# A four-layer conditioning sum in 1024-column pieces, merged weight sums, 24 more weight units by seven products, and all three short-convolution taps of two layers on ScalarE

## The reference, cut to what matters

```python
# first stack, layer i
g, u = jnp.split(h @ w_up[i], [D_FF], axis=-1)          # D_FF = 2816
g = depthwise_conv_centered(g, ffn_conv_w[i], ffn_conv_b[i])   # 3 taps
x = x + (jax.nn.silu(g) * u) @ w_down[i]

# second stack, layer i
def adaln(c, w, b):                                     # w is 1024 x 6144, one per layer
    m = jax.nn.silu(c) @ w + b
    return [t[:, None, :] for t in jnp.split(m, 6, axis=-1)]

def conv_ffn(h, w_up, conv_w, conv_b, w_down):          # gate and value are both convolved
    u = causal_dwconv(h @ w_up, conv_w, conv_b)         # 3 taps over 2 * 2816 channels
    gate, val = jnp.split(u, 2, axis=-1)
    return (jax.nn.silu(gate) * val) @ w_down
```

## Time and profile before

| | us |
|---|---|
| median of three runs | 2409.67 (2407.22 to 2412.18) |
| span of the profiled execution, first to last instruction | 2408.9 |
| PE busy (17412 matmul records) | 2386.9 (99%) |
| DVE busy | 1625.6 (67%) |
| ACT busy | 717.3 (30%) |
| POOL busy | 154.4 (6%) |
| conditioning loads by POOL, 96 of 1024 KB, median from issue to landing | 7.5 |

### The profile page before, as it was taken

One profiled execution on the slowest core, in us unless ns is written; L12 is line 12 of the kernel. 1 busy time (PEld: TensorE's weight loads), 2 busy tenths in 40 slices (PEclk: granted clock), 3 DMA queues, 4 the chain that ended last, 5 costly groups with the idle time before them and its releaser, 6 DMA issues.

```text
span 2408.9 us, 41954 instructions
## 1 busy us (share of the span) xinstructions
PE 2386.9 (99%) x17412; PEld 2184.3 (91%) x17412; DVE 1625.6 (67%) x3307; ACT 717.3 (30%) x1445; POOL 154.4 (6%) x268
## 2 busy tenths in 40 slices
PE   9999999999999999999999999999999999999998
PEld 7879999987899998999998899898899999989998
DVE  6653887566289847688744389954477984638983
ACT  3442211144312121433132233223433431544321
POOL 2000110000021000001000031011000000000000
PEclk9999999999999999999999999999999999999999
DMA  7935995474399746589454399744334555335442
GB/s 218 242 90 177 338 306 197 141 191 122 106 325 318 250 149 189 189 311 307 160 172 139 106 336 317 242 149 123 108 118 160 168 170 167 110 107 173 162 164 97
DMA packets 403272, 458.40 MB, mean 190 GB/s; under 512 B 50751, under 2 KB 374776, under 8 KB 403084
## 3 DMA queue, kind: packets, MB, share of 16 engines
q1 hardware_dynamic: 370098, 340.53, 45.1%
q0 software_dynamic: 29936, 112.73, 12.9%
q10 hardware_dynamic: 3050, 2.46, 0.4%
HBM read 451.48 MB, written 1.29 MB: 188 GB/s over the span
## 4 chain that ended last, share of the span: by engine, by line
PE 93%; DVE 4%; DMA 1%; issue 1%; ACT 0%; POOL 0%; DVEq 0%; POOLq 0%
PE job_bank L1021 37%; PE job_bank L1097 28%; PE job_bank L1076 11%; PE mix_bank L1076 4%; PE job_bank L1606 4%; PE job_bank L1105 1%; PE mix_bank L1553 1%; PE job_bank L1581 1%; PE mix_bank L1525 1%; DVE sb_arena L3047 1%; PE mix_bank L1567 1%; DVE sb_arena L3091 0%; PE mix_bank L1052 0%; PE mix_bank L1897 0%; PE job_bank L1329 0%
## 5 line engine op out<-in xcount | busy, mean ns | idle before, releaser
L1021 PE MATMUL job_bank<-sb_h,sb_ring 128*128 128x256 f32 (+1 forms) x3456 | 770.3, 380 | 0.7 <-DVE sb_h L3324 0.7
L1021 PEld LDWEIGHTS job_bank<-sb_h,sb_ring 128*128 128x128 f32 (+1 forms) x3456 | 644.9, 189 | 95.0 <-issue 9.2
L3047 DVE SCALAR_TENSOR_TENSOR sb_arena<-sb_arena,sb_c_act 128x512 f32<-128x512 f32 x336 | 252.7, 752 | 10.6
L3154 DVE SCALAR_TENSOR_TENSOR sb_arena<-sb_arena,sb_par 128x256 f32<-128x256 f32 x440 | 204.6, 506 | 9.2 <-ACT sb_arena L2179 5.3
L1076 PE MATMUL job_bank<-sb_h,sb_ring 128*128 128x128 f32 x1600 | 184.1, 275 | 1.4 <-ACT sb_h L2482 1.4
L1076 PEld LDWEIGHTS job_bank<-sb_h,sb_ring 128*128 128x128 f32 x1600 | 181.2, 192 | 1.8 <-issue 1.6
L1097 PE MATMUL job_bank<-sb_t,sb_ring 128*128 128x128 f32 x1248 | 165.5, 275 | 0.0
L2179 ACT ACTIVATE sb_arena<-sb_arena,sb_par 128x256 f32<-128x256 f32 x220 | 120.2, 593 | 119.0 <-DVE sb_arena L3122 117.8
L1097 PE MATMUL job_bank<-sb_h,sb_ring 128*128 128x128 f32 x1152 | 152.8, 276 | 0.0
L1097 PEld LDWEIGHTS job_bank<-sb_t,sb_ring 128*128 128x128 f32 x1248 | 152.2, 192 | 0.0
L1097 PE MATMUL job_bank<-sb_arena,sb_ring 128*128 128x128 f32 x1216 | 151.9, 275 | 0.0
(11 more groups left out here) (519 smaller groups left out, 3362.9 us busy)
## 6 DMA issues: line engine op xcount, KB each, us to landing
sb_arena<-in_ada_w POOLq DMA_DIRECT2D x96, 1024.0 KB, 7.5
sb_ring<-in_ffn_w_up SPq DMA_DIRECT2D x88, 1024.0 KB, 5.3
sb_ring<-in_w_up SPq DMA_DIRECT2D x44, 1024.0 KB, 6.7
sb_ring<-in_ffn_w_down SPq DMA_DIRECT2D x32, 1024.0 KB, 5.0
sb_ring<-in_w_in SPq DMA_DIRECT2D x24, 1024.0 KB, 6.1
sb_ring<-in_w_down SPq DMA_DIRECT2D x16, 1024.0 KB, 5.0
sb_ring<-in_hg_w_in SPq DMA_DIRECT2D x16, 1024.0 KB, 5.5
sb_ring<-in_ml_w_up SPq DMA_DIRECT2D x16, 1024.0 KB, 5.4
```

The costliest lines, as they stand in the source:

```text
L1021: mm = pe.matmul(o, st, mv, start=(k0 + k == 0 and t == 0), stop=(k0 + k == kn - 1), skip_group_check=True)
L3047: ins = vec.scalar_tensor_tensor(out=o, in0=w, scalar=col, in1=o, op0=ALU.mult, op1=ALU.add)
L3154: ins = vec.scalar_tensor_tensor(out=o, in0=fraw[:, i % 2, v, j:j + T], scalar=pcol(column, (l * FFN_TAPS + j) * width + c), in1=o, op0=AL ...
```

## The change

Five things are changed together. (1) Conditioning units become 2 row tiles by 1024 columns, still 1 MB and 24 per layer: two multiply-adds of 1024 columns each in `ada_unit`. The ring of four buffers becomes three buffers for units 0 to 14 and two (buffers 1 and 2 in turn) for units 15 to 23. 15 units are consumed beside the 22 up jobs, 2 after d0 has been added to x, 2 after the forms of d2's units, and 5 after the join of d1. (2) The six quads now follow up jobs 9, 15 and 21, then one stands where two stood among d2's products, one ahead of the last products of d2's third unit, and one right behind them. (3) `weight_forms` takes three operations, the last of 1024 columns making two blocks at once; the third quarter of a fast unit now waits for that last one (`form_last`). (4) 24 more up units are fast: values 1, 3, 5, 7, 9 in both first-stack parts, and gates 1, 4, 7, 10 and values 3, 6, 9 in layers 0 and 1 of the second stack; `FAST_VALUES` names the values. (5) In those two second-stack layers ACT computes all three taps (`all_taps`, six activations of 256 columns for two tiles) and DVE only adds them up (`add_taps`, two additions of 512 columns). Places of buffers move accordingly, and the copies of middle banks alternate between two buffers.

```diff
-ADA_RING = 4
-ADA_PARTS = 10
+ADA_RING = 3
+ADA_COLS_AT_ONCE = 4 * UC
 PAIRS = NH // 2
 ADA_COLS = 6 * D // P
 ADA_UNITS = 6 * D // UC
+ADA_BESIDE_UP = 15
 FAST_FROM = 2
-FAST_PAIRS = (2, 3, 5, 6, 8, 9)
+FAST_VALUES = {1: (1, 3, 5, 7, 9), 2: (3, 6, 9)}
 FORMS = 3
...
+        spare_at = ffn.at
+        ffn(8 * UC)
+        ada_w = ffn(ADA_RING, 2, ADA_COLS_AT_ONCE)
+        ada_part = ffn(2, ADA_COLS_AT_ONCE)
         ada_rows = ffn(UC)
+        ada_buffer = [c % 3 if c < ADA_BESIDE_UP else 1 + (c + 1) % 2 for c in range(ADA_UNITS)] * L2
+        ada_before = [max((m for m in range(n) if ada_buffer[m] == b), default=None) for n, b in enumerate(ada_buffer)]
+        ada_landed = [16 * ada_buffer[:n + 1].count(b) for n, b in enumerate(ada_buffer)]
...
+        def form_place(s2, pair_in, pair_at, apart=quarter_n):
+            both = pair_in[:, pair_at:pair_at + 2 * apart].rearrange("p (f n) -> p f n", f=2)[:, :, 0:quarter_n]
+            return s2.rearrange("p (k c) -> p k c", c=P), both.rearrange("p f (k c) -> p f k c", c=P)
...
+        cond_slots = [in_row(spare_at), in_row(spare_at + 3 * quarter_n),
+                      form_place(h_flat[:, 0:quarter_n], h_flat, quarter_n),
+                      form_place(h_last, arena, spare_at + 6 * quarter_n)]
...
-            if stack == 2 and l >= FAST_FROM:
-                return [job for both in zip(gates[1:], values[1:]) for job in both]
-            return gates[1:] if stack == 1 else [gates[i] for i in FAST_PAIRS]
+            return [job for i in range(1, FT // 2) for job in (gates[i], values[i])
+                    if job is gates[i] or stack == 2 and l >= FAST_FROM or i in FAST_VALUES[stack]]
...
-                    if n >= ADA_RING:
-                        pool.wait_ge(s.ada_acc, n - ADA_RING + 1)
-                    src = a["ada_w_2"][layer][c % 2 * D // 2:(c % 2 + 1) * D // 2, c // 2 * 2 * UC:(c // 2 + 1) * 2 * UC]\
+                    if ada_before[n] is not None:
+                        pool.wait_ge(s.ada_acc, ada_before[n] + 1)
+                    src = a["ada_w_2"][layer][c % 4 * 2 * P:(c % 4 + 1) * 2 * P,
+                                              c // 4 * ADA_COLS_AT_ONCE:(c // 4 + 1) * ADA_COLS_AT_ONCE]\
                         .rearrange("(k p) c -> p k c", p=P)
-                    pool.dma_start(ada_w[:, n % ADA_RING, :, :], src).then_inc(ada_in[n % ADA_RING], 16)
+                    pool.dma_start(ada_w[:, ada_buffer[n], :, :], src).then_inc(ada_in[ada_buffer[n]], 16)
...
-                pe.wait_ge(s.form_first, 2 * f + 1)
+                pe.wait_ge(s.form_first, f + 1)
                 pe.wait_ge(s.tform_ready, n_t + 1)
-                quarter(bank[:, 1, :], form_slot(unit)[0][:, 0:kt // 2, :], forms[:, 0, :, :])
-                pe.wait_ge(s.form_first, 2 * f + 2)
+                quarter(bank[:, 1, :], a21, forms[:, 0, :, :])
+                pe.wait_ge(s.form_last, f + 1)
                 pe.wait_ge(s.tform_ready, n_t + 2)
-                mm = quarter(bank[:, 2, :], a21, forms[:, 2, :, :])
+                mm = quarter(bank[:, 2, :], form_slot(unit)[1][:, 1, 0:kt // 2, :], forms[:, 2, :, :])
...
-                    if n in (9, 17):
-                        ada_quad()
+                    if n in (9, 15, 21):
                         ada_quad()
...
                 ada_quad()
-                ada_quad()
                 tail = half_steps(d3, row_of, 0)
                 fill(tail, 2 * KD)
-                for u in range(3):
+                for u in range(2):
                     last_products(d2, u, *over_f(u))
+                ada_quad()
+                last_products(d2, 2, *over_f(2))
+                ada_quad()
                 for mm in tail:
                     pass
                 mm.then_inc(s.half_done, 1)
...
+            def all_taps(l, i, q, joined=None):
+                if joined:
+                    read_out(act, joined)
+                    if q == 0 and i >= 2:
+                        products(act, 2, l, i - 2)
+                if q and i:
+                    products(act, 2, l, i - 1)
+                for v in (q, q + 1):
+                    w, b = tap_column(2, l, i, v, 0)
+                    step(act.activation(fcv[:, i % 2, v, :], fraw[:, i % 2, v, 0:T], ACT.Identity, bias=b, scale=w))
+                for v in (q, q + 1):
+                    w, _ = tap_column(2, l, i, v, 1)
+                    step(act.activation(tap_sums[:, q // 2, v % 2, :], fraw[:, i % 2, v, 1:1 + T], ACT.Copy, scale=w))
+                settle()
+                for v in (q, q + 1):
+                    w, _ = tap_column(2, l, i, v, 2)
+                    row = fraw[:, i % 2, v, 2:2 + T]
+                    ins = act.activation(row, row, ACT.Copy, scale=w)
+                ins.then_inc(s.tap_ready, 1)
...
+                held = None
+                def finish():
+                    i, q, job = held
+                    if stack == 2:
+                        all_taps(l, i, q, job)
+                    elif q == 0:
+                        first_tap(stack, l, i, q, job)
+                for i in range(FT // 2):
+                    for q, job in ((0, gates[i]), (2, values[i])):
+                        if job[0] in fast_no:
+                            keep_mid(job)
+                        if held:
+                            keep_corner(held[2])
+                        if q == 0 and i:
                             gate(i - 1)
-                    if stack == 2:
-                        raw_out(stack, l, i, 2, u)
-                        first_tap(stack, l, i, 2)
-                        if 0 < i <= KD:
-                            scale_x(l, i - 1)
+                        if held:
+                            finish()
+                            held = None
+                        if job[0] in fast_no:
+                            held = i, q, job
+                        elif stack == 2:
+                            raw_out(stack, l, i, q, job)
+                            all_taps(l, i, q)
+                        elif q == 0:
+                            raw_out(stack, l, i, q, job)
+                            first_tap(stack, l, i, q)
+                    if stack == 2 and 0 < i <= KD:
+                        scale_x(l, i - 1)
...
+            def ada_unit():
+                n = ada_n[0]
+                vec.wait_ge(ada_in[ada_buffer[n]], ada_landed[n])
+                if n % 4 == 0 and n >= 8:
+                    vec.wait_ge(s.ada_summed, n // 4 - 1)
+                o = ada_part[:, n // 4 % 2, :]
+                for k in range(2):
+                    w = ada_w[:, ada_buffer[n], k, :]
+                    col = c_act[:, n % 4 * 2 + k:n % 4 * 2 + k + 1]
+                    if n % 4 == 0 and k == 0:
...
-                f = [v[:, 0:kt // 2, :] for v in form_slot(unit)]
+                a11, _, a21, a22 = corners(unit, kt)
+                n = kt // 2
+                right = slot(unit)[:, n:kt, :].rearrange("p k (g c) -> p g k c", c=P)
+                s2, both = form_slot(unit)
                 vec.wait_ge(unit_in[unit % RING], landed[unit])
+                vec.tensor_tensor(a21, a21, a22, ALU.add).then_inc(s.form_first, 1)
+                own(s.form_first, form_no[unit] + 1)
                 form_free(vec, unit)
-                vec.tensor_tensor(f[0], a21, a22, ALU.add).then_inc(s.form_first, 1)
-                own(s.form_first, 2 * form_no[unit] + 1)
-                vec.tensor_tensor(a21, a11, a21, ALU.subtract).then_inc(s.form_first, 1)
-                step(vec.tensor_tensor(f[1], f[0], a11, ALU.subtract))
-                settle()
-                vec.tensor_tensor(f[2], a12, f[1], ALU.subtract).then_inc(s.form_last, 1)
+                step(vec.tensor_tensor(s2[:, 0:n, :], a21, a11, ALU.subtract))
+                settle()
+                vec.tensor_tensor(both[:, :, 0:n, :], right, s2[:, 0:n, :].unsqueeze(1).to_broadcast([P, 2, n, P]),
+                                  ALU.subtract).then_inc(s.form_last, 1)
...
+            def add_taps(i, q):
+                o = fcv[:, i % 2, q:q + 2, :]
+                vec.wait_ge(s.tap_ready, due(s.tap_ready))
+                step(vec.tensor_tensor(o, o, tap_sums[:, q // 2, :, :], ALU.add))
+                settle()
+                ins = vec.tensor_tensor(o, o, fraw[:, i % 2, q:q + 2, FFN_TAPS - 1:FFN_TAPS - 1 + T], ALU.add)
+                if q == 0:
+                    ins.then_inc(s.gconv_ready, 1)
+                    due(s.gconv_ready)
+                else:
+                    step(ins)
...
+                ups = [job for both in zip(gates, values) for job in both]
+                def ahead(p):
+                    if p < len(ups) and ups[p][0] in fast_no:
+                        more_forms(1)
+                def beside(p):
+                    ada_units((p + 1) * ADA_BESIDE_UP // len(ups) - p * ADA_BESIDE_UP // len(ups))
+                ahead(2)
...
-                    ada_half()
+                    ahead(2 * i + 3)
```

(57 more changed lines are left out.)

100 lines of the change are left out of this document (40 added, 60 removed).

## The result

The changed kernel takes 2471.3 us (median of four runs, 2470.0 to 2474.3) against 2409.2 us before (median of four runs): ratio 1.0257, 95% interval 1.0242 to 1.0271. The profiled execution has a span of 2468.7 us against 2408.9, so 59.8 us more are to be found in it.

A forecast was written before the change was run, and what follows sets the result against it. PE's instruction stream was taken as the bound (busy 2386.9 of 2408.9 us). Fast units -16.0, waits +45.5, clock +6.8 and ACT +4 sum to +40.3: 2449.2 on the profile, 2450 us on the median; range 2418 to 2482.

The forecast's parts named there:

- A: Rival, down part: reloads are not what DVE waits for, landings below some 2.5 us; faster, 2402 us; chance 0.08.
- D: Rival, down part: a small loss with landings between 4 and 5 us; 2415 to 2424 us; chance 0.06.
- B: Rival, up part: no wait at the quads, but fast units give nothing as DVE or ACT runs late; about 2409; chance 0.04.
- C: Rival: ACT and DVE late in every second-stack pair and loads at 8.3 us; +79, 2489 us; chance 0.10.
- The wait: Down part: PE waits at the last quad for DVE's reloads, 11.4 us (first stack), 11.3 (second); four parts, +45.5 us.
- 11.4 + 3 x (L - 6.5): Wait ahead of the last quad, three landings in series; L is issue to landing, 6.5 us taken; bounds 7.8 to 14.4.
- The clock: Behind each of the four waits: a stretch at the lower clock level costs 1.7 us, +6.8 in all.
- The fast units: Up parts: 24 more fast units save 0.67 us each on PE's path, -16.0 us.
- ACT in the second stack: Up parts of the second stack: PE waits for ACT behind the taps, 2 us a part, +4 for two parts.
- Nothing for DVE in the up part: Up part: DVE keeps up with PE, 11.1 us a pair against 12.8 (second stack 11.4 against 12.9), so costs nothing.

The follow-up runs named there:

- e2: Changed kernel with three conditioning buffers in place of two in the second stack's down part: 2462.4 us (1.0219 of the kernel before).
- e1: Changed kernel with half of the data left out of the last five conditioning loads of each conditioned part: 2452.7 us (1.0185 of the kernel before).
- e6: Changed kernel with 17 conditioning units beside the up phase in place of 15, seven in the down part: 2420.4 us (1.0047 of the kernel before).
- e8: e3 without the 24 more fast units, which are computed plainly as in the kernel before: 2414.7 us (1.0019 of the kernel before).
- e3: Changed kernel with 19 conditioning units beside the up phase in place of 15, five in the down part: 2402.9 us (0.9974 of the kernel before).
- e7: e3 with the second stack's taps split as before the change, one on ACT and two on DVE: 2402.9 us (0.9974 of the kernel before).
- e9: e3 with seven fast values in place of five in each first-stack part: 2410.5 us (1.0005 of the kernel before).

## Why the prediction was right, and where its sizes were off

The forecast was 2450 us, the range 2418 to 2482, the result 2471.3. The mechanism, the place and the count of the waits were as told, and the four rivals fall: A and D needed landings under 5 us where those in series took 5.7 to 9.1, B no wait, C ACT late in every pair and landings of 8.3 us. (The prediction's "no load here landed under 5.3 us" holds for the conditioning loads; 1 MB weight loads of the same trace have medians near 5.0.) The 21 us between forecast and result are mostly sizes, term by term:

- **The wait, +45.5 forecast, +61.9 measured.** This is the term that was mis-sized. In the first stack PE reached the last quad at 430.9, which is 431.6 on the time axis of before (the part starts 0.7 us earlier now); the forecast was 430.5. The formula 11.4 + 3 x (L - 6.5) holds: the three landings in series came to 22.2 us, 7.4 each, in place of 6.5, which gives 14.1 against 14.3 (in layer 1 they are 7.2 each, 13.6 against 14.9). The median of the two loads of one stretch was the wrong choice; the median of all loads, 7.5, in the same rows gave the upper bound of 14.4. In the second stack the forecast (11.3) missed 15.9 and 16.9, and this is 10.2 of the 16.4 us. On the time axis of before DVE ended its chain in layer 0 at 1222.8, not at 1218.8. More than half of this is that the forms of d2's last unit ended 2.4 us later than I had them: I let them follow PE's lead, and their weight load was indeed issued earlier, but it took 8.0 us in place of 4.3 (e2). The formula with three landings does not hold there either: by my own layout unit 19 lands at 1197.9, before DVE is free, so only two stand in series, and I used three for the bounds of all four parts. e1 and e2 together show both halves, since smaller loads took 3.7 us out of a wait there and a third buffer 6.
- **The clock, +6.8 forecast, +8.5 measured.** Near; but e6 shows that for the waits ahead of this quad the price hardly depends on their length (8.2 us for waits of 1.7 to 3.7). The prediction has the burst start at the half rate. That is so behind the long waits; in the earlier trace rows and in e6's first stack it starts at full clock and falls 0.7 to 1.4 us later.
- **The fast units, -16.0 forecast.** e8 against e3: 11.8 us net of 3.8 us of waits that come with them, so 15.6 by the medians and, with a difference of 10.2, 14.0 by the profiled spans. In the parts without waits it is 0.65 a unit, forecast 0.67.
- **ACT in the second stack, +4 forecast as 2 a part.** Measured 0 in layer 0 and 3.0 in layer 1. The place was right (the copy of the next gate's middle products behind the taps of a held value). But ACT starts these taps only when DVE has joined that value, and ahead of one of the two waits an addition of DVE takes 2.05 us in place of 0.69 beside a POOL operation. Only layer 1 has POOL operations beside its up part. With one tap on ACT 1.4 us of wait remain (e7), so the taps are not its only cause; the shares were not tried.
- **Nothing for DVE in the up part.** Right, and by more than I used: DVE also took four more units there (e3).
- **Not forecast:** quads that stand alone (24, at 0.14 us at most, so some 3 us) and 1.7 us of waits for a weight load and its forms in the last down part; and the 5.1 us that come back outside the parts. Of these 1.6 are a wait for DVE, in the mixer behind the first part, and 1.7 the half-rate stretch of the earlier trace rows; the changed kernel has neither, though PE waits 2.0 us ahead of that stretch in it too. That the pieces that were not forecast cancel is luck.

The Trainium skill, DMA: Bandwidth & Descriptors, section Anatomy of one DMA, gives an estimate of 4.4 us a load. Of the conditioning loads in e1 the quickest of 0.5 MB took 4.0 us and the quickest of 1 MB 5.4: 1.4 us for the second half, about what that page's rate gives (1.2, an estimate), but over a fixed part of 2.6 rather than 2.0. With others in flight the landings in series took up to 9.1 us. The quickest landing is no price for a reload in series.

## What to carry to other kernels

When work is moved out of a stretch where it was hidden, count the buffers it has at its new place: two buffers and a reload that waits for a consumption put landings in series, and each costs its full latency beside the other loads (5.7 to 9.1 us here). Size such a chain by the landings' overall median, count for each part which landings are really waited for, and ask separately whether the engine in front would be in time without them. Ask also what the moved loads do to the loads that were there before. Before paying for the move, see whether the engine was full where the work came from: here DVE was idle for about a fifth of it, and four units put back turned +2.6% into -0.26%.

## What the runs showed of the hardware that I had not expected

- A short wait can cost as much clock as a long one. PE idle for 1.7 us was followed by work at half rate that cost 1.6 us (e6), PE idle for 14.3 us by 2.9 and for 14.9 us by 1.4. It need not cost any: the waits of 1.5 us in the changed kernel's last up part left the granted clock at 1.00, and so did one of 2.0 us where the kernel before lost 1.7.
- VectorE instructions can be stretched beside GpSimd's. A 128x512 product of two tensors on VectorE took 0.69 us alone and 2.58 beside a GpSimd tensor_tensor of 1.97 (e9); the gap, 1.89, is nearly that instruction's length. The Trainium skill, SBUF — State Buffer, section SBUF: two separate sides, says that the pair of ports the two engines share is locked for a whole instruction; the trace agrees in the length of the stretch. Which of the two had the ports first it doesn't tell, since VectorE's row begins 0.05 us ahead of GpSimd's.
- Halving a conditioning load of 1 MB took its quickest landing from 5.4 to 4.0 us only (e1).
